# One decoder step in two passes: the last head's choice moved across the pass boundary, two gating tiles moved across a stage boundary, and the norms' scale and bias put on two engines

## What is computed

```python
def trunk(x, ...):
    proj = x @ w_in
    z, xbc, dt_raw, uv, gates = split(proj)
    y_a = ssd_branch(z, xbc, dt_raw, ...)      # causal conv, chunked scan, rms norm of each group
    y_b = chunk_sgu_branch(uv, ...)            # u * (W_s layer_norm(gelu(v)) + b), in chunks of 128
    merged = sigmoid(g_a) * (y_a @ w_branch_a) + sigmoid(g_b) * (y_b @ w_branch_b)
    h = layer_norm(ALPHA * x + merged @ w_out, ln1_g, ln1_b)
    return layer_norm(ALPHA * h + peer(h, ...), ln2_g, ln2_b)

def peer(h, w_q, sub_keys, u_tab, v_tab):
    q = h @ w_q                                # 8 heads, two sides of 128 numbers each
    s = scores of both sides against 128 keys
    top_s, top_i = top_k(s, 16)                # of each side
    best_s, best_c = top_k(all 256 sums, 16)   # 16 experts of each head
    expert, gate = numbers(top_i, best_c), softmax(best_s)
    return sum over the 128 experts of gate * gelu(h . u_tab[expert]) * v_tab[expert]
```

## Time and profile before

| | |
|---|---|
| median of 3 runs | 5128.65 us (5126.14 to 5131.64) |
| the profiled execution | 5127.28 us, of which its span is 5125.0 us |
| PE busy | 4510.0 us (88%) |
| DVE busy | 2815.0 us (55%) |
| POOL busy | 2244.2 us (44%) |
| ACT busy | 857.9 us (17%) |
| DMA moved | 1674.50 MB, mean 327 GB/s |
| first pass | scan to about 687 us, gating to 943, back to 1800 |
| second pass | scan to about 2587, gating to 2860, back to about 3750 |
| tail | from about 3750 us to the end |

### The profile page before, as it was taken

The page is one execution under the profiler, slowest core; times in us unless marked ns, Lnnn a source line. Parts: engine busy times, 40 slices in busy tenths (PEclk is TensorE's granted clock), DMA queues, the critical chain, the costliest instruction groups (busy, mean ns, idle before and its releaser), DMA issues. The chain is left out here.

```text
span 5125.0 us, 48494 instructions
## 1 busy us (share of the span) xinstructions
PE 4510.0 (88%) x18494; PEld 3359.0 (66%) x18494; DVE 2815.0 (55%) x3723; ACT 857.9 (17%) x1941; POOL 2244.2 (44%) x1637
## 2 busy tenths in 40 slices
PE   8999999999999987887889899899857777887776
PEld 6888878888887776776778788787733322332222
DVE  3565622000002778888867865566886655464445
ACT  2333311100000133333301110000111111110000
POOL 3676640000000335554543623454588875364442
PEclk9999999999999998998999999999979999899999
DMA  6767654445554589999999999999999999999998
GB/s 205 231 216 224 210 189 131 136 148 165 165 176 135 171 330 399 416 417 408 417 384 419 417 416 416 384 417 417 376 421 421 421 422 419 382 419 422 422 421 364
DMA packets 331806, 1674.50 MB, mean 327 GB/s; under 512 B 47200, under 2 KB 62112, under 8 KB 195872
## 3 DMA queue, kind: packets, MB, share of 16 engines
q0 software_dynamic: 160640, 1133.71, 54.1%
q1 hardware_dynamic: 165768, 536.51, 30.2%
q10 hardware_dynamic: 5168, 1.19, 0.1%
HBM read 1633.31 MB, written 37.89 MB: 326 GB/s over the span
## 5 line engine op out<-in xcount | busy, mean ns | idle before, releaser
L596 PE MATMUL psum<-rows_a,w_ring 128*128 128x264 f32 x6656 | 1503.4, 388 | 13.2 <-PEq L551 8.8
L596 PEld LDWEIGHTS psum<-rows_a,w_ring 128*128 128x128 f32 x6656 | 1265.6, 191 | 236.0 <-issue 20.9
L596 PE MATMUL psum<-x_and_spare,w_ring 128*128 128x256 f32 x5632 | 1259.7, 384 | 49.6 <-PEq L1511 13.9
L596 PEld LDWEIGHTS psum<-x_and_spare,w_ring 128*128 128x128 f32 x5632 | 1076.8, 193 | 218.8 <-issue 61.0
L404 POOL DMA_INDIRECT rows_a<-in_peer_u,expert x384 | 721.7, 1880 | 888.4 <-DVE rows_a L459 824.0
L459 DVE SCALAR_TENSOR_TENSOR rows_a<-rows_a,h_tokens 128x2048 f32<-128x2048 f32 x388 | 888.3, 2291 | 330.2 <-DMA rows_a<-in_peer_u,expert 304.9
L404 POOL DMA_INDIRECT rows_a<-in_peer_v,expert x382 | 515.9, 1350 | 371.1 <-PE psum L503 169.2
L503 PE MATMUL psum<-rows_b,diags 128*128 128x512 f32 x1008 | 480.0, 625 | 179.9 <-ACT diags L493 130.0
L503 PE MATMUL psum<-rows_a,diags 128*128 128x512 f32 x1008 | 485.7, 630 | 153.2 <-ACT diags L493 100.2
L503 PEld LDWEIGHTS psum<-rows_b,diags 128*128 128x128 f32 x1008 | 191.4, 198 | 466.3 <-issue 296.4
L503 PEld LDWEIGHTS psum<-rows_a,diags 128*128 128x128 f32 x1008 | 193.6, 200 | 445.5 <-issue 302.9
(11 more groups left out here) (385 smaller groups left out, 3375.6 us busy)
## 6 DMA issues: line engine op xcount, KB each, us to landing
w_ring<-in_w_tiles SPq DMA_DIRECT2D x896, 512.0 KB, 6.0
rows_a<-in_state_ssm POOLq DMA_DIRECT2D x32, 512.0 KB, 5.7
out_ssm_sample<-rows_a POOLq DMA_DIRECT2D x32, 512.0 KB, 4.5
rows_a<-acum_rows_dram SPq DMA_DIRECT2D x16, 512.0 KB, 5.2
rows_a<-smp_bc_dram POOLq DMA_DIRECT2D x8, 1024.0 KB, 8.1
acts_by_token<-late SPq DMA_DIRECT2D x16, 512.0 KB, 6.7
branch_b<-acum_rows_dram SPq DMA_DIRECT2D x16, 512.0 KB, 12.8
rows_a<-in_xT SPq DMA_DIRECT2D x3, 2048.0 KB, 13.6
```

Source lines behind the costliest of these rows:

```text
L596: last = pe.matmul(o, w[:, k * P:(k + 1) * P], x[:, k, :], start=start and k == 0, stop=stop and k == KB - 1)
```

## The change

Three edits, and a helper.

1. **Head 7.** The first pass's back stage leaves out the selection of head 7; its scores stay in two banks of the accumulation memory. The second pass's scan begins on DVE with that selection, ahead of the first convolution, and ACT does the exponentials behind the first evacuation. Head 6 now takes the way that head 7 had: DVE works out its numbers and shares itself (`last_numbers`), and POOL's turn for it goes.
2. **Gating's first two tiles.** In the first pass PE projects v tiles 0 and 1 at the end of the scan's block, one before the last `rms`, one after it. Their outputs are read out by ACT in the gating's block, as before.
3. **Norms.** In all four norms DVE multiplies each block with g and the inverse root in one instruction, and ACT adds b (`ln_bias`). In the gating ACT does four blocks, then reads out u tiles 0 and 1, then does the other twelve.

```diff
@@ ssd, second pass: names
+        if ps.i == 1:
+            ranked, aord, picked_exp = S_("last_ranked", "act", "last_exp")
+            top = Selection(self.region(spare), slice(0, P), PASS_CHUNKS[0][1], self.iota)
@@ ssd, tensor, after the last group
+                if ps.smp:
+                    project(G, 0)
                 rms(G - 1)
+                if ps.smp:
+                    project(G, 1)
@@ ssd, scalar
                 evac(0, 0)
                 if ps.i == 0:
                     make["decays"](act)
+                else:
+                    act.wait_ge(ranked, 1)
+                    top.exps(Chain(act, aord), act, PH - 1).then_inc(picked_exp, 1)
@@ ssd, vector
+                if ps.i == 1:
+                    blocks, p = range(top.nb), PH - 1
+                    for side in range(2):
+                        top.top16(o, dve, [self.bank[4 + side][:, b * P:(b + 1) * P] for b in blocks],
+                                  [top.spare[:, b] for b in blocks], [top.tv[:, b, side] for b in blocks],
+                                  [top.ti[p % 2][:, b, side] for b in blocks])
+                    top.ranked(o, dve, p, ranked)
+                    dve.wait_ge(ranked, 1)
+                    self.last_numbers(dve, o, top, p, picked_exp, 1)
                 conv(0, 0)
@@ ln_scale and the new ln_bias
-        for c in range(4):
-            w = v[:, 4 * c:4 * c + 4, :]
-            dve.tensor_tensor(w, w, mid(root[:], 1, 4), ALU.mult).then_inc(s["inv"], 1)
-            dve.wait_ge(s["inv"], c + 2)
-            for k in range(4 * c, 4 * c + 4):
-                dve.tensor_scalar(v[:, k, :], v[:, k, :], g[:, k:k + 1], b[:, k:k + 1],
-                                  ALU.mult, ALU.add).then_inc(s["normed"], 1)
+        for k in range(KB):
+            dve.scalar_tensor_tensor(out=v[:, k, :], in0=v[:, k, :], scalar=g[:, k:k + 1], in1=root[:],
+                                     op0=ALU.mult, op1=ALU.mult).then_inc(s["scaled"], 1)
+
+    def ln_bias(self, act, v, b, s, first, count):
+        for k in range(first, first + count):
+            act.wait_ge(s["scaled"], k + 1)
+            act.activation(v[:, k, :], v[:, k, :], ACT.Identity, bias=b[:, k:k + 1]).then_inc(s["normed"], 1)
@@ sgu, tensor and scalar
-                    project(m)
+                    if m >= 2 or not ps.smp:
+                        project(m)
...
                 self.ln_root(act, ps, root, ln)
+                self.ln_bias(act, v, self.lnp[:, 1, :], ln, 0, 4)
                 gelu_u(0)
                 gelu_u(1)
+                self.ln_bias(act, v, self.lnp[:, 1, :], ln, 4, KB - 4)
@@ back, pool: one head fewer; scalar: the bias, and no last exp
-                    elif m % 2 == 1:
-                        if p < PH - 1:
+                    elif m % 2 == 1 and p < PH - 1:
+                        if p < PH - 2:
                             heads(p)
...
+                self.ln_bias(act, h, self.lnp[:, 3, :], ln, 0, KB)
...
-                if not pick:
-                    exp(PH - 1)
@@ back, vector
-                for m in range(0 if pick else FT):
+                for m in range(0 if pick else FT - 2):
...
+                    self.last_numbers(dve, o, top, PH - 2, exp_done, PH - 1)
+    def last_numbers(self, dve, o, top, p, exp_done, count):
+        every = slice(TOPK * p, TOPK * (p + 1))
+        o(top.places(o, dve))
+        top.key_numbers(o, dve, p)
+        top.picked_keys(o, dve)
+        dve.wait_ge(self.head_done, p)
+        o(top.pair_numbers(o, dve))
+        dve.tensor_copy(self.eid[:, 0:top.nb, every], top.number).then_inc(self.head_done, 1)
+        dve.wait_ge(exp_done, count)
+        o(top.inverse(dve, p))
+        dve.wait_ge(self.gate_done, p)
+        top.shares(dve, p, self.gates[:, 0:top.nb, every]).then_inc(self.gate_done, 1)
```

More of the change, by code:

```diff
@@ L1416, in ln_sems @@
     def ln_sems(self, name, by_vector):
-        return {m: self.sem(f"{name}_{m}") for m in ("in", "mean", "square", "summed", "centred", "root", "inv", "normed")
+        return {m: self.sem(f"{name}_{m}") for m in ("in", "mean", "square", "summed", "centred", "root", "inv", "scaled", "normed")
                 + (("added", "folded") if by_vector else ())}
@@ L1472, in ln_centre, with ln_scale @@
             dve.tensor_tensor(w, w, mid(self.bank[2][:, 0:ps.n], 1, 4), ALU.subtract).then_inc(s["centred"], 1)
-    def ln_scale(self, dve, v, root, g, b, s):
+    def ln_scale(self, dve, v, root, g, s):
         dve.wait_ge(s["centred"], 4)
@@ L1651, in _ @@
                     self.ln_fold(dve, o, yb, ln)
-                self.ln_scale(dve, v, root, self.lnp[:, 0, :], self.lnp[:, 1, :], ln)
+                self.ln_scale(dve, v, root, self.lnp[:, 0, :], ln)
                 dve.wait_ge(b_in, 16)
@@ L2025, in _ @@
                 experts("ln", 0)
-                self.ln_scale(dve, h, root, self.lnp[:, 2, :], self.lnp[:, 3, :], ln)
+                self.ln_scale(dve, h, root, self.lnp[:, 2, :], ln)
                 experts("ln", 1)
@@ L2054, in _ @@
                             top.inverse(dve, p - 1).then_inc(inverted, 1)
-                        if p < PH - 1:
+                        if p < PH - 2:
                             top.places(o, dve).then_inc(picked, 1)
                 if not pick:
-                    last = slice(TOPK * (PH - 1), TOPK * PH)
-                    o(top.places(o, dve))
-                    top.key_numbers(o, dve, PH - 1)
-                    top.picked_keys(o, dve)
-                    dve.wait_ge(self.head_done, PH - 1)
-                    o(top.pair_numbers(o, dve))
-                    dve.tensor_copy(self.eid[:, ps.c0:ps.c0 + top.nb, last], top.number).then_inc(self.head_done, 1)
-                    dve.wait_ge(exp_done, PH)
-                    o(top.inverse(dve, PH - 1))
-                    top.shares(dve, PH - 1, self.gates[:, ps.c0:ps.c0 + top.nb, last]).then_inc(self.gate_done, 1)
+                    self.last_numbers(dve, o, top, PH - 2, exp_done, PH - 1)
[11 more added lines that the diff above has]
+        top.shares(dve, p, self.gates[:, 0:top.nb, every]).then_inc(self.gate_done, 1)
     def tail(self, acc0, ex):
```

## The result

| | before | after |
|---|---|---|
| median of 5 runs | 5131.64 us (5126.14 to 5134.26) | 5105.71 us (5101.39 to 5107.35) |
| the profiled execution's span | 5125.0 us | 5102.6 us |
| PE busy | 4510.0 us | 4506.7 us |
| DVE busy | 2815.0 us | 2798.0 us |
| ACT busy | 857.9 us | 883.1 us |

The ratio of the times is 0.9948, with a 95% interval of 0.9936 to 0.996: 26.7 us faster, between 20 and 33. The predicted gain was 26.4 us. The two profiled spans differ by 22.4. Nothing was saved in work: the same matmuls and the same bytes. ACT has 25 us more to do, DVE 17 less. What was won is mostly time in which PE stood still (span less PE busy: 615.0 before, 595.9 after).

What follows compares the result with a forecast made beforehand. PE was taken to bound the first pass, full DMA engines the second pass and tail. Terms 11.5 + 11.5 + 1.5 + 3.4 - 1.0 - 0.5 = 26.4 us, taken from 5128.65, gave 5102.3; range 5093 to 5114.

Steps and rivals of the forecast that it cites:

- Head 7: Boundary of the passes: with head 7's selection moved to the second pass, PE starts 11.55 us earlier; taken as 11.5.
- a lag that is not taken up: Second pass's start: if the convolutions' delay of 6.9 us is not made up, 4.6 us of gain is left.
- 1 to 3 us to spare: Second pass's scan: PE's first tiles cover the moved selection, so PE waits for nothing, with 1 to 3 us of slack.
- Gating's tiles: First pass, scan's end: two gating tiles around the last rms sum fill PE's pauses; 11.5 us won (8.6 to 13.7).
- second rival: Gating's start: tiles only trade the barrier wait for one on tile 2's bank and weights; 5121 us; chance 0.08.
- The fourth weight tile: First pass's gating: tile 3's load, asked for late, comes at 705 where PE wants it at 701.7; up to 3.3 us less.
- First pass, back norm: First pass's back stage: the query tile starts 0.9 us earlier and no longer waits for the last group; +1.5 us (0.9 to 3.5).
- Second pass, back norm: Second pass's back stage: the chain of waits runs over DVE, so its 3.5 us come through; +3.4 us (0 to 3.5).
- First pass, gating norm: First pass's gating: PE's tile starts 1.9 us later, behind four biases and a table load; -1.0 us (-1.9 to +0.5).
- The third rival: Second pass's start: the selection crawls beside POOL, at 7.1 times its length; kernel slower, 5200 us; chance 0.04.
- The table loads: Gatings: no drain of about 1380 ns per table switch was counted; with it the gain would be 22 us in all.
- Second pass, gating norm: Second pass's gating: the same loss as in the first pass's gating, but under full DMA engines; -0.5 us (-1.9 to 0).

## Why the prediction was right, point by point

- **The time.** 5102.3 was predicted, 5105.71 came, and 5103.0 is the mean of 16 runs. In us gained: 26.4 predicted, 26.7 by the ratio (20 to 33), 28.7 by the mean of the three ratios. Of the 3.4 between the two times, 3.0 are the kernel before, whose median went from 5128.65 (3 runs) to 5131.64 (5 runs). That the sum came out within 0.3 us is partly luck: the interval is some 12 us wide, and terms that were too high (both gating norms) made up for others that were too low.
- **Head 7** (11.5 predicted): 11.8 at the boundary, by both comparisons. The range's lower end, 4.6 for a lag that is not taken up, is excluded by the doubled selection. The step's slack was mis-sized: "1 to 3 us to spare" took the evacuations of tiles 1 and 2 as due when the tile ended. Each is due only when PE wants that bank again, when the next tile has ended too; about 9 us were to spare, and tile 1, behind ACT's wait for the selection, is the one that runs out first. Undone alone the edit costs more than the 11.8, and 3 to 5 us of that stay open.
- **Gating's tiles** (11.5, from 8.6 to 13.7): 12.0 in the first trace, and from 10.8 to 13.7 over the others, by the clock of tile 2. The new wait was counted as 3.1 and is 2.92, where two waits of 11.7 stood, so the prediction's second rival falls. The fourth weight tile was not late.
- **First pass, back norm** (1.5, from 0.9 to 3.5). From the root's start to the query copy it was 14.11 with the old norm in both traces; with the new one 11.04 in six traces and 13.6 to 13.7 in six. So it is 3.1 or 0.4, by the clock of one tile, and 1.75 in the mean. The step "it then takes about 9 us" held one value where there are two, and the smaller gain lies below the range.
- **Second pass, back norm** (3.4). DVE gained 3.9, and 3.7 of it (standard error 1.9) reaches the end. The doubt after the first two traces, in which 3.9 seemed to shrink to 0.5, came from the scatter of the tail.
- **First pass, gating norm** (-1.0, from -1.9): -2.0, just outside. The failing step is "before, PE waited 0.6 behind it for ACT; ACT is done earlier now": the later start was to be paid back by that wait. The wait did go, but the tile behind the longer pause took 9.91 in place of 8.97, and that used it up (8.8 to 10.1 in nine traces with this order, 8.97 in all three with the old norm). The loss came from the order on ACT, and goes with it.
- **The third rival.** The selection ran from 1778.35 to 1794.94, 16.6 us, beside 16.8 on the other side of the boundary, so there was no crawl. POOL's four gathers were issued between 1778.99 and 1783.73, beside the maxima; the two-input products ran later, when POOL stood idle, and were not put to the test.
- **The table loads.** In the runs the next activation stands directly behind the load: loads end at 814.89 and 684.90, and the activations start at 814.91 and 684.91. The Trainium skill, "ScalarE: Activation LUTs" (What ACT_TABLE_LOAD costs), gives a drain of about 1380 ns with each switch of tables; the runs disagree with it.
- **Second pass, gating norm** (-0.5, from -1.9): about -2.3, outside the range. The failing step is "the same loss, but under full DMA engines": the loss is not regained there. The first u tile starts 6.81 behind the root's end and 4.28 before (the lines are below). From the root's start to the first centring of the back norm it is 871.14 in the kernel before and 871.34 after, which looks like nothing lost. All traces say otherwise: 868.9 to 871.7, mean 870.4, in the five whose u tiles 0 and 1 are read out ahead of any bias, and 871.3 to 875.0, mean 872.7, in the nine with four biases ahead (standard error of the difference 0.6). The DMA share in the gating is 1.02, yet behind the first u tile PE waits there only for ACT's last two copies (0.46 each) and at the barrier (13.89), the same in both traces, and for no transfer. So the expectation of the undone norms, and that of the u tiles first, had this wrong too. Whether the 2.3 us reach the end is not shown: no median tells a term of that size.

```profile
2730.63 0.47 ACT L1466 ACTIVATE v_root<-psum,eps 128x256 f32<-128x256 f32 x1 [1.32 <-PE psum L1454]
...
2735.39 9.11 PE L596 MATMUL psum<-x_and_spare,w_ring 128*128 128x256 f32 x32
```

```profile
2708.34 0.47 ACT L1485 ACTIVATE v_root<-psum,eps 128x256 f32<-128x256 f32 x1 [0.72 <-PE psum L1473]
...
2715.62 9.86 PE L596 MATMUL psum<-x_and_spare,w_ring 128*128 128x256 f32 x32 [2.21 <-ACT branch_b L1620]
```

## What to carry to other kernels

Time that PE stands still in a stage which it bounds can be won by putting another stage's tiles there, if the bank and the weights are free (here 12.0 us, for two pauses of 11.7, a new one of 2.92 and a faster clock). Count the cover to the moment when PE wants a bank again, not to the end of the tile that fills it. When work moves to an engine that is nearly idle, look at what its program has next: here four biases ahead of two gelus cost 2 us in each pass, and one gelu ahead of the squares 5.6, on an engine that is busy 17% of the time. Full DMA engines did not take up a loss where PE waited for no transfer (2.3 us in the second gating). Where runs scatter by 4 us, a term of 3 us is read from the same stretch in many traces, not from two.

## What the runs showed of the hardware that was not expected

The same tile behind the same pause runs at either clock. Behind the 2.92 us at the gating's start, ten traces show 6.97 us from the end of one read-out to the start of the next in three, 8.5 to 8.7 in six and 9.92 in one; behind the 3.68 us at the first query tile, 7.36 in half of twelve and some 10 in the other half (granted clock 1.00 and 0.72, that is 2.4 GHz for the whole tile, or 1.2 for a part of it). Three such places in the first pass (gating tile 2, the first gate, the first query tile) differ by up to 2.9, 1.6 and 2.7 us between traces of nearly the same program. A prediction can give such a term as two values and a chance, no better.
